# Seven of the last convolution tile's 31 taps made on TensorE as products with diagonal matrices

## The chip, the cores and the metric

The program runs on one core of one Trainium2 chip. The metric is the device time of one execution in microseconds (us). Engines: PE is TensorE, DVE is VectorE, ACT is ScalarE, POOL is GpSimd, and SP is SyncE, which issues the DMAs here. PE's clock has two levels, 1.2 and 2.4 GHz; the profile gives the granted clock as a share of the higher one (PEclk 0.50 or 1.00).

## What is computed

A trunk of two layers over 512 latent and 256 context tokens of width 1024. Layer 0 mixes tokens with a Conformer convolution module, layer 1 with windowed attention; behind each stands a mixture of experts. The change lies in the convolution module of layer 0:

```python
CONV_WIDTH = 31
def depthwise_conv(u, w, b, pad):
    y = lax.conv_general_dilated(u, w[:, None, :].astype(u.dtype), window_strides=(1,), padding=[pad],
                                 dimension_numbers=('NWC', 'WIO', 'NWC'), feature_group_count=u.shape[-1])
    return y + b.astype(u.dtype)

def conformer_conv(h, pw1, pw1_b, dw, dw_b, ln_g, ln_b, pw2, pw2_b):
    u = h @ pw1 + pw1_b
    u = u[..., :D_MODEL] * jax.nn.sigmoid(u[..., D_MODEL:])
    half = (CONV_WIDTH - 1) // 2
    u = depthwise_conv(u, dw, dw_b, (half, half))
    u = jax.nn.silu(layernorm(u, ln_g, ln_b))
    return u @ pw2 + pw2_b
```

Each channel is convolved along the tokens with its own 31 weights, all in float32. The layer norm behind it needs the mean and the variance over all 1024 channels, so its first step can't end before the last channel's convolution has.

## The kernel before

The channels lie on the partitions. There are 8 tiles (`KT`) of 128 channels, and a row of a tile has 783 columns (`CONVW`): 256 of context, a gap of 15, and 512 latent ones. Each engine has its own program, and semaphores order them.

**Pairs and loops.** Tiles go in pairs, `j` = 0 and 1 of pair `i` = 0 to 3. Pair 0 is written out; pairs 1 to 3 are a loop in each engine's program (`Fori`), where addresses and semaphore values come from registers.

**DVE.** `both_glu` (two instructions of L1302) multiplies the gate into the padded tile `UP`. `taps` then makes 31 instructions over 783 columns, one a tap: L1316, L1319, then 29 of L1321. Even taps add up in the tile's row block of `V` (shown as AR), odd ones in `ACC2` (shown as ROWS), and L1342 adds the two and raises `conv_done`. `mod_columns` follows the last tile (L443, L451: ten small instructions on the modulation columns), then eight of L1371 subtract the mean (`centred`).

**PE.** Per pair the pointwise product (`first_conv`, L1201), then `sum_mods`: five chunks of the modulation weights, each 2 MB by DMA into a slot of `RING`, as 32-column products (L426) and small ones that turn the sums (L433). After the loop stand the channel sums of tiles 0 to 5 (`add_mean`, L1225, two matmuls a tile: 512 and 271 columns with a matrix of ones), the last `sum_mods`, the channel sums of tiles 6 and 7, two transposes (`mod_rows_turn`, L457), and the sums of squares of all 8 tiles (L1249).

**ACT.** Sigmoids, the copies of the modulation sums out of PSUM (`copy_part`, L1258), then the squares (L1285), a square root (L1287) and the SiLU (L1290).

After the norm, L1377 (mean square out of PSUM), L1380 (reciprocal) and L1383 (scale, `scaled`) run on DVE; PE starts the second pointwise product (L861) with ACT's results, and SP starts six row loads (L470) and the first expert weights (L710) behind `scaled`. L1064 on DVE takes the first of those rows.

PSUM columns 1024 to 1806 (banks 2 and 3) hold the sums of squares (`VAR`) and, earlier, some modulation sums. Slot 2 of `RING` holds the second modulation chunk of each pair.

Of the kernel before, what the change touches and what calls it, by code (L numbers as in the profile page):

```python
# [24 lines left out]
P = 128  # L25
# [101 lines left out]
def build(nc, a, out):  # L127
    with ExitStack() as stack:
# [161 lines left out]
        pw_in = [sem(f"pw_in{j}") for j in range(2)]  # L290
        ctx_summed = sem("ctx_summed")
        ctx_sig_done = sem("ctx_sig_done")
        gate_summed = sem("gate_summed")
        val_summed = sem("val_summed")
        sig_done = sem("sig_done")
# [852 lines left out]
        VAR = PSF[:, 1024:1024 + CONVW]  # L1148
        NSTEP = 2 * (1 + TAPS)
        PART_BANK = (6, 2, 6, 2, 6)  # L1150


        MODS = [(0, 2 * KT + 4 * c, 2) for c in range(2)] + [(1, 4 * c, 3) for c in range(3)]
# [6 lines left out]
        with nc.Block() as block:  # L1160
# [32 lines left out]
            @block.tensor  # L1193
            def _(pe):
                def first_conv(i, j):
                    pe.wait_ge(pw_in[j], i * 32 + 32)
                    pe.wait_ge(glu_done[j], i + 1)
                    for (t0, lat, n, _), u, done in ((segs[0], 0, None), (segs[0], 1, ctx_summed),
                                                     (segs[1], 0, gate_summed), (segs[1], 1, val_summed)):
                        for k in range(KT):  # L1200
                            ins = pe.matmul(conv_bank(j, u, lat), PWB[:, j, u, k, :], HT[:, k, t0:t0 + n],  # L1201
                                            start=(k == 0), stop=(k == KT - 1))
                        if done:
                            ins.then_inc(done, 1)

                def add(i, c):
                    L, at, m = MODS[c]
                    pe.wait_ge(part_copied, i * 5 + (5 + c))
                    mod_rows_add(pe, L, i * (4 * m) + at, c)

                def sum_mods(i):
                    if not isinstance(i, int):
                        pe.wait_ge(glu_done[0], i + 3)
                    for c in range(len(MODS)):
                        if c >= 2:
                            add(i, c - 2)
                        pe.wait_ge(modB_in[c], i * 16 + (32 if c < 4 else 16))
                        mod_rows_sum(pe, PART_BANK[c], slot(1 + c, KT))
                    for c in range(len(MODS) - 2, len(MODS)):
                        add(i, c)  # L1220

                def add_mean(f):
                    pe.wait_ge(conv_done, f + 2)
                    for c0, c1 in ((0, 512), (512, CONVW)):
                        ins = pe.matmul(MEAN[:, c0:c1], ones[:, :], V[:, f, c0:c1], start=(f == 0), stop=(f == KT - 1))  # L1225
                    return ins

                for j in range(2):
                    first_conv(0, j)
                with pe.Fori(1, KT // 2) as i:  # L1230
                    for j in range(2):
                        first_conv(i, j)
                    sum_mods(i - 1)
                pe.wait_ge(glu_done[0], KT // 2 + 1)
                for f in range(KT - 2):
                    add_mean(f)
                sum_mods(KT // 2 - 1)
                pe.wait_ge(part_turned, 5 + 4 * len(MODS))
                pe.sem_inc(mod_summed[1], 1)
                for f in range(KT - 2, KT):  # L1240
                    ins = add_mean(f)
                ins.then_inc(mean_summed, 1)
                mod_rows_turn(pe, 0)
                mod_rows_turn(pe, 1)

                for f in range(KT):
                    pe.wait_ge(squared, f + 1)
                    for c0, c1 in ((0, 512), (512, CONVW)):
                        ins = pe.matmul(VAR[:, c0:c1], ones[:, :], SQ[:, f % 2, c0:c1],  # L1249
                                        start=(f == 0), stop=(f == KT - 1))  # L1250
                    ins.then_inc(sq_used, 1)

            @block.scalar
            def _(act):
                def copy_part(i, c):
                    act.wait_ge(part_summed, i * 5 + (5 + c))
                    act.wait_ge(part_turned, i * 5 + (1 + c))
                    nc.scalar.activation(PARTS[:, c, :], PS[:, PART_BANK[c], :], ACT.Copy).then_inc(part_copied, 1)  # L1258

                def sigmoid(i, j, seg, done):  # L1260
                    t0, lat, n, _ = seg
                    nc.scalar.activation(SGT[:, j, t0:t0 + n], conv_bank(j, 0, lat), ACT.Sigmoid,
                                         bias=cols[:, bass.ds(i * 2 + (VC["conv_pw1_b"] + KT + j), 1)]).then_inc(done, 1)

                def gates(i):
                    for j in range(2):
                        act.wait_ge(ctx_summed, i * 2 + (j + 1))
                        act.wait_ge(glu_done[j], i + 1)
                        sigmoid(i, j, segs[0], ctx_sig_done)
                        act.wait_ge(gate_summed, i * 2 + (j + 1))  # L1270
                        act.sem_inc(act_step, 1)
                        sigmoid(i, j, segs[1], sig_done)

                gates(0)
                with act.Fori(1, KT // 2) as i:
                    gates(i)
                    for c in range(len(MODS)):
                        copy_part(i - 1, c)
                for c in range(len(MODS)):
                    copy_part(KT // 2 - 1, c)  # L1280
                for f in range(KT):
                    act.wait_ge(centred, f + 1)
                    if f >= 2:
                        act.wait_ge(sq_used, f - 1)
                    nc.scalar.activation(SQ[:, f % 2, :], V[:, f, :], ACT.Square).then_inc(squared, 1)  # L1285
                act.wait_ge(var_ready, 1)
                nc.scalar.activation(STD, STD, ACT.Sqrt).then_inc(std_ready, 1)  # L1287
                for f in range(KT):
                    act.wait_ge(scaled, f + 1)
                    nc.scalar.activation(V[:, f, :], V[:, f, :], ACT.Silu,  # L1290
                                         scale=cols[:, VC["conv_ln_g"] + f:VC["conv_ln_g"] + f + 1],
                                         bias=cols[:, VC["conv_ln_b"] + f:VC["conv_ln_b"] + f + 1]).then_inc(z_ready, 1)

            @block.vector
            def _(dve):
# [49 lines left out]
                def first_tile(n):  # L1345
# [10 lines left out]
                    nc.vector.tensor_tensor(vf, vf, more, ALU.add).then_inc(conv_done, 1)  # L1356
                    return n

                n = first_tile(1)
                n = tile(0, 1, 0, n)  # L1360
                with dve.Fori(1, KT // 2) as i:
                    base = dve.snap(i * NSTEP + (n - NSTEP))
                    m = tile(i, 0, base, 0)
                    tile(i, 1, base, m)
                dve.wait_ge(mod_summed[1], 1)
                mod_columns(dve, 0, 2, NMOD)
                mod_columns(dve, 1, 0, NMOD)
# [799 lines left out]
```

## Time and profile before

| | us |
|---|---|
| median of 3 runs | 1571.44 |
| lowest, highest | 1570.62, 1572.45 |
| the profiled execution | 1571.96 |
| its span | 1570.2 |
| PE busy | 1348.2 |
| DVE busy | 757.1 |
| ACT busy | 508.3 |

Time points are us from the span's start. The convolution module takes the stretch to about 357 us. PE's share of the whole says little about it: there DVE is busy almost without a break and PE waits.

A float32 matmul is shown as two MATMUL and two LDWEIGHTS records, so the four matmuls of two channel sums are x8. In a merged row of the timeline the duration runs from the first start to the last end.

### The profile page before, as it was taken

Reading aid. Unit: us, or ns where it says so; the run is one execution under the profiler, and the core shown is the slowest. Engines: PE = TensorE matmul, PEld = TensorE weight load, DVE = VectorE, ACT = ScalarE, POOL = GpSimd, SP = SyncE. Lnnn points to the kernel's source line nnn. Section 1 sums busy time; section 2 is a strip of 40 time slices with the busy share of each in tenths; the row PEclk is TensorE's granted clock in tenths of the full one; section 3 lists DMA queues with packets and bytes.
Section 4 is the critical chain, followed back from the end, with each engine's and each line's share of the span. In section 5 each row is a group of like instructions: output and inputs, shape, how many; then the busy total and the mean of one; then the engine's idle time right before and its main releaser. Section 6 shows DMA issues by size and latency. Waiting matters only on the chain. (4 is left out here: it accounts for less than half of the span.)

```text
span 1570.2 us, 22957 instructions
## 1 busy us (share of the span) xinstructions
PE 1348.2 (86%) x6818; PEld 625.1 (40%) x6819; DVE 757.1 (48%) x1405; ACT 508.3 (32%) x783; POOL 126.7 (8%) x176
## 2 busy tenths in 40 slices
PE   4899998477978899999998299799998698998980
PEld 2555563234443233333332144378744332332320
DVE  2699999955773221221211541366647342232215
ACT  3101000042323443443332330166523253453423
POOL 0000000000320010010100200000002100100002
PEclk9999999778988999999999699899999799999995
DMA  9825473616049999699633500050094899999915
GB/s 345 286 73 198 156 268 136 251 59 252 40 181 341 396 398 375 238 329 333 240 116 126 216 0 0 5 104 1 1 335 144 307 337 395 397 370 397 359 33 194
DMA packets 163826, 342.97 MB, mean 218 GB/s; under 512 B 9104, under 2 KB 34304, under 8 KB 163776
## 3 DMA queue, kind: packets, MB, share of 16 engines
q1 hardware_dynamic: 146448, 298.29, 52.5%
q0 software_dynamic: 7440, 25.43, 4.4%
q10 hardware_dynamic: 9888, 18.62, 3.5%
q8 instruction: 27, 0.44, 0.1%
q14 instruction: 23, 0.19, 0.0%
HBM read 312.07 MB, written 30.24 MB: 218 GB/s over the span
## 5 line engine op out<-in xcount | busy, mean ns | idle before, releaser
L1485 PE MATMUL PS<-WR,XT 128*64 128x512 f32 x1760 | 414.1, 614 | 29.8 <-DVE WR L1618 20.2
L1485 PEld LDWEIGHTS PS<-WR,XT 128*64 128x64 f32 x1760 | 127.5, 140 | 266.0 <-issue 208.2
L1630 DVE TENSOR_TENSOR HID<-PS,SIL 64x512 f32<-64x512 f32 x55 | 37.5, 682 | 393.6 <-ACT SIL L1562 393.6
L1498 PE MATMUL PS<-WR,HTT 128*64 128x512 f32 x880 | 204.6, 608 | 9.5 <-ACT HTT L1567 9.5
L1551 ACT ACTIVATE WR<-WR 128x2048 f32 x90 | 169.0, 1906 | 100.5 <-issue 88.9
L1201 PE MATMUL PS<-HT,RING 128*128 128x512 f32 (+1 forms) x512 | 169.3, 494 | 6.5 <-DVEq L1299 6.5
L1618 DVE COPY WR<-WR 128x2048 f32 x90 | 107.0, 1224 | 97.9 <-PE PS L1498 40.3
L1201 PEld LDWEIGHTS PS<-HT,RING 128*128 128x128 f32 x512 | 99.4, 195 | 74.2 <-issue 66.3
L1321 DVE SCALAR_TENSOR_TENSOR AR<-AR,cols 128x783 f32 (+3 forms) x135 | 126.5, 937 | 0.0
L1321 DVE SCALAR_TENSOR_TENSOR ROWS<-AR,cols,ROWS 128x783 f32<-128x783 f32 (+2 forms) x126 | 118.0, 936 | 0.0
L1498 PEld LDWEIGHTS PS<-WR,HTT 128*64 128x64 f32 x880 | 59.4, 139 | 110.1 <-issue 106.6
L861 PE MATMUL PS<-RING,AR 128*128 128x512 f32 x192 | 93.0, 627 | 9.3 <-ACT AR L1290 9.3
L1799 PE MATMUL PS<-RING,HT 128*128 128x512 f32 x224 | 99.7, 603 | 1.3 <-ACT ROWS L1836 1.3
L1562 ACT ACTIVATE SIL<-PS 64x512 f32<-64x512 f32 x55 | 32.7, 594 | 116.4 <-PE PS L1485 116.4
L2040 DVE CUSTOM_DVE_ANT_0 HT<-PS,AR 128x512 f32<-128x512 f32 (+1 forms) x64 | 49.8, 815 | 33.9 <-PE PS L1964 33.9
L426 PE MATMUL PS<-RING,sc 128*32 128x512 f32 x384 | 51.8, 670 | 14.2 <-DMA RING<-in_w_mod 9.2
L1799 PEld LDWEIGHTS PS<-RING,HT 128*128 128x128 f32 x224 | 42.8, 194 | 52.9 <-issue 52.9
L861 PE MATMUL PS<-RING 128*128 128x512 f32 x128 | 60.2, 614 | 2.5 <-PEq L1940 2.5
L1574 ACT ACTIVATE YO<-PS 128x512 f32<-128x512 f32 x55 | 32.3, 587 | 89.6 <-PE PS L1498 89.6
L715 POOL DMA_INDIRECT XG<-moe_in,icur x57 | 55.7, 977 | 42.7 <-POOL icur L1451 41.5
L1567 ACT ACTIVATE HTT<-PS 128x256 f32<-128x256 f32 x55 | 20.6, 375 | 109.1 <-issue 59.9
L944 POOL TENSOR_SCALAR AR<-CN,HT 128x64 f32<-128x64 f32 x16 | 15.3, 959 | 501.8 <-DVEq L1035 501.8
(234 smaller groups left out, 1307.4 us busy)
## 6 DMA issues: line engine op xcount, KB each, us to landing
WR<-in_moe_w SPq DMA_DIRECT2D x192, 1024.0 KB, 15.6
RING<-in_w_mod SPq DMA_DIRECT2D x24, 2048.0 KB, 15.0
moe_out<-YO ACTq DMA_DIRECT2D x110, 128.0 KB
RING<-in_conv_pw SPq DMA_DIRECT2D x16, 512.0 KB, 5.4
moe_out<-HT SPq DMA_DIRECT2D x16, 512.0 KB, 8.7
ROWS<-rows_of_layer SPq DMA_DIRECT2D x12, 512.0 KB, 6.0
RING<-in_attn_w_qkv SPq DMA_DIRECT2D x3, 2048.0 KB, 8.5
RING<-in_conv_pw SPq DMA_DIRECT2D x2, 2048.0 KB, 9.7
```

Source lines behind the costliest of these rows:

```text
L426: ins = pe.matmul(PS[g:g + 32, bank, :], sc2[:, k, :], w[:, k, :], start=(k < 4), stop=(k >= 4), tile_position=(0, g))
L715: pool.indirect_dma_start(out=XG[:, :], out_offset=None, in_=src, in_offset=bass.IndirectOffsetOnAxis(ap=icur[:, 0:1], axis=0)).then_inc(x ...
L861: ins = pe.matmul(PS[:, 2 * (i % 2) + h, :], lhs(i, k), weights(k)[:, h * 512:(h + 1) * 512], start=(k == 0), stop=(k == KT - 1))
L1201: ins = pe.matmul(conv_bank(j, u, lat), PWB[:, j, u, k, :], HT[:, k, t0:t0 + n], start=(k == 0), stop=(k == KT - 1))
L1321: ins = nc.vector.scalar_tensor_tensor(out=to, in0=u, scalar=w, in1=to, op0=ALU.mult, op1=ALU.add)
L1485: ins = pe.matmul(PUV[g * SUB:(g + 1) * SUB, :], XT[:, k, :], w[:, k * FE:(k + 1) * FE], start=(k == 0), stop=(k == KT - 1), tile_position ...
L1498: ins = pe.matmul(PYO[c * SUB:(c + 1) * SUB, :], HTT[:, k, :], W2[:, at:at + 512], start=(k == 0), stop=(k == FE // P - 1), tile_position= ...
L1551: return nc.scalar.activation(to, src, ACT.Copy)
L1618: return nc.vector.tensor_copy(to, src)
L1630: nc.vector.tensor_tensor(HID[:, :], PUV[0:SUB, :], SIL[:, :], ALU.mult).then_inc(hid_ready[L], 1)
L1799: ins = pe.matmul(PS[:, bank, :], HT[:, k, t * P:(t + 1) * P], slot(QKV_SLOT[c], KT)[:, k, :], start=(k == 0), stop=(k == KT - 1))
L2040: nc.vector.tensor_tensor_reduce(out=SS[:, 2 * (s % 3) + b, 0:w], in0=PSF[:, 1024 * b:1024 * b + w], in1=mask, scale=-DH ** -0.5, scalar=n ...
```

## The change

Taps 24 to 30 of the last tile (pair 3, `j` = 1) leave DVE. ACT writes seven diagonal matrices of 128 by 128 (`DIAG`, in slot 2 of `RING`), each the identity scaled by that tap's weight column. PE multiplies each with the shifted 783 columns of `UP`, two matmuls a tap, and adds them up in PSUM banks 2 and 3 (`TAPSUM`). DVE makes 24 taps, adds its two accumulators, waits for `taps_summed`, and adds `TAPSUM`; that second addition raises `conv_done`.

To give the last tile a form of its own, DVE's loop now ends with pair 2, and pair 3 is written out. PE's and ACT's loops are as before.

```diff
+        PE_TAPS = 7
+        DIAG = RING[:, 2, 0:PE_TAPS * P].rearrange("p (k n) -> p k n", k=PE_TAPS)
+        TAPSUM = PSF[:, 1024:1024 + CONVW]
...
                 pe.sem_inc(mod_summed[1], 1)
-                for f in range(KT - 2, KT):
-                    ins = add_mean(f)
+                add_mean(KT - 2)
+                pe.wait_ge(ctx_sig_done, KT + 1)
+                pe.wait_ge(glu_done[1], KT // 2 + 1)
+                for k in range(PE_TAPS):
+                    at = TAPS - PE_TAPS + k
+                    for c0, c1 in ((0, 512), (512, CONVW)):
+                        ins = pe.matmul(TAPSUM[:, c0:c1], DIAG[:, k, :], UP[:, 1, at + c0:at + c1],
+                                        start=(k == 0), stop=(k == PE_TAPS - 1))
+                ins.then_inc(taps_summed, 1)
+                ins = add_mean(KT - 1)
                 ins.then_inc(mean_summed, 1)
...
                 for c in range(len(MODS)):
                     copy_part(KT // 2 - 1, c)
+                for k in range(PE_TAPS):
+                    w = DW + (TAPS - PE_TAPS + k) * KT + KT - 1
+                    ins = nc.scalar.activation(DIAG[:, k, :], ident, ACT.Copy, scale=cols[:, w:w + 1])
+                ins.then_inc(ctx_sig_done, 1)
...
+                def last_tile(n):
+                    i, j = KT // 2 - 1, 1
+                    n = both_glu(i, j, 0, n)
+                    n, (vf, more) = taps(i, j, 0, n, 0, CONVW, TAPS - PE_TAPS)
+                    nc.vector.tensor_tensor(vf, vf, more, ALU.add).then_inc(conv_step, 1)
+                    dve.wait_ge(conv_step, n + 1)
+                    dve.wait_ge(taps_summed, 1)
+                    nc.vector.tensor_tensor(vf, vf, TAPSUM, ALU.add).then_inc(conv_done, 1)
...
-                with dve.Fori(1, KT // 2) as i:
+                with dve.Fori(1, KT // 2 - 1) as i:
                     base = dve.snap(i * NSTEP + (n - NSTEP))
                     m = tile(i, 0, base, 0)
                     tile(i, 1, base, m)
+                n += (KT // 2 - 2) * NSTEP
+                n = tile(KT // 2 - 1, 0, 0, n)
+                last_tile(n)
```

PE, behind the last modulation chunk (L433 before, L434 in the change). Before, the channel sums of tiles 6 and 7 (L1225) and the two transposes (L457):

```order
L433 MATMUL PS<-CN,ROWS 128x2 x3
L1225 MATMUL PS<-AR,ones 128x512 [waits mod_part_turned,conv_done]
L1225 MATMUL PS<-AR,ones 128x271
L1225 MATMUL PS<-AR,ones 128x512 [waits conv_done]
L1225 MATMUL PS<-AR,ones 128x271
L457 MATMUL PS<-CN,modc 96x128 [waits mod_cols0]
```

The change, the same place (L1229 is the channel sum, L1250 a tap; 14 rows of L1250 in all):

```order
L434 MATMUL PS<-CN,ROWS 128x2 x3
L1229 MATMUL PS<-AR,ones 128x512 [waits mod_part_turned,conv_done]
L1229 MATMUL PS<-AR,ones 128x271
L1250 MATMUL PS<-AR,RING 128x512 [waits glu_done1,ctx_sig_done]
L1250 MATMUL PS<-AR,RING 128x271
...
L1250 MATMUL PS<-AR,RING 128x512
L1250 MATMUL PS<-AR,RING 128x271
L1229 MATMUL PS<-AR,ones 128x512 [waits conv_done]
L1229 MATMUL PS<-AR,ones 128x271
```

Between the two channel sums now stand 14 matmuls, ahead of the one that waits for the last tile.

DVE, the end of the last tile. Before, the last two taps (L1321) with a register instruction ahead of each, the sum of the accumulators (L1342), the loop's branch, and `mod_columns` (L443):

```order
L1311 REGISTER_ALU
L1321 ISA [waits conv_step]
L1321 SCALAR_TENSOR_TENSOR ROWS<-AR,cols,ROWS 128x783
L1311 REGISTER_ALU
L1321 ISA [waits conv_step]
L1321 SCALAR_TENSOR_TENSOR AR<-AR,cols 128x783
L1325 REGISTER_ALU
L1342 TENSOR_TENSOR AR<-AR,ROWS 128x783 [waits conv_step]
L1361 REGISTER_ALU
L1361 COMPARE_AND_BRANCH
L443 TENSOR_TENSOR modc<-PS,cols 128x32 [waits mod_summed1]
```

The change, the same place (L1337 is a tap, L1379 the sum of the accumulators, L1382 the addition of PE's part):

```order
L1337 SCALAR_TENSOR_TENSOR AR<-AR,cols 128x783 [waits conv_step]
L1337 SCALAR_TENSOR_TENSOR ROWS<-AR,cols,ROWS 128x783 [waits conv_step]
L1379 TENSOR_TENSOR AR<-AR,ROWS 128x783 [waits conv_step]
L1382 TENSOR_TENSOR AR<-AR,PS 128x783 [waits taps_summed,conv_step]
L444 TENSOR_TENSOR modc<-PS,cols 128x32 [waits mod_summed1]
```

The register instructions are gone, and one addition with a wait for PE has come.

## Rows read from the trace of the kernel before

**Rows 1.** Waits by engine and line, 255 to 360 us: total, times, longest

```profile
PE PS L1225 <- DVE AR L1342: 17.5, 1, 17.5
...
DVE RING L1064 <- DMA ROWS<-rows_of_layer: 11.8, 1, 11.8
...
DVE ROWS L1377 <- PE PS L1249: 6.1, 1, 6.1
...
DVE AR L1371 <- PE PS L1225: 1.1, 1, 1.1
```

**Rows 2.** Timeline of DVE, last tile, in the loop: start, duration, line

```profile
281.69 1.14 DVE L1302 SCALAR_TENSOR_TENSOR AR<-PS,cols,ROWS 128x256 f32<-128x256 f32 x2
283.20 0.69 DVE L1316 TENSOR_SCALAR AR<-AR,cols 128x783 f32 x1 [0.37 <-DVE AR L1302]
284.04 0.63 DVE L1319 TENSOR_SCALAR ROWS<-AR,cols 128x783 f32<-128x783 f32 x1 [0.15 <-DVE AR L1316]
284.58 1.03 DVE L1321 SCALAR_TENSOR_TENSOR AR<-AR,cols 128x783 f32 x1
...
311.03 1.03 DVE L1321 SCALAR_TENSOR_TENSOR AR<-AR,cols 128x783 f32 x1
312.10 0.97 DVE L1342 TENSOR_TENSOR AR<-AR,ROWS 128x783 f32 x1
```

**Rows 3.** Timeline of DVE, the second tile, written out, and the next tile's start

```profile
94.28 1.14 DVE L1302 SCALAR_TENSOR_TENSOR AR<-PS,cols,ROWS 128x256 f32<-128x256 f32 x2
96.72 1.03 DVE L1321 SCALAR_TENSOR_TENSOR AR<-AR,cols 128x783 f32<-128x783 f32 x1
...
125.14 1.14 DVE L1302 SCALAR_TENSOR_TENSOR AR<-PS,cols,ROWS 128x256 f32<-128x256 f32 x2
```

**Rows 4.** Timeline of PE, 268 to 341 us

```profile
268.55 8.15 PE L1225 MATMUL PS<-AR,ones 128*128 128x512 f32 x24
...
290.00 1.92 PE L426 MATMUL PS<-RING,sc 128*32 128x512 f32 x16 [2.45 <-DMA RING<-in_w_mod]
...
293.95 1.67 PE L1225 MATMUL PS<-AR,ones 128*128 128x512 f32 x4
313.12 2.98 PE L1225 MATMUL PS<-AR,ones 128*128 128x512 f32 x4 [17.50 <-DVE AR L1342]
315.89 0.63 PE L457 MATMUL PS<-CN,modc 128*96 128x128 f32 x2
318.05 13.02 PE L1249 MATMUL PS<-AR,ones 128*128 128x512 f32 x32 [1.53 <-ACT AR L1285]
340.36 10.14 PE L861 MATMUL PS<-RING,AR 128*128 128x512 f32 x16 [9.28 <-ACT AR L1290]
```

**Rows 5.** Busy time by stretch: length, PE, PEld, DVE, ACT, POOL; then PEclk, DMA share, GB/s

```profile
148.50:151.90 3.40, 3.40 (x10) 2.65 (x9) 3.40 (x5) 0.00 (x0) 0.00 (x0) 0.50 1.04 386
...
246.60:250.80 4.20, 0.00 (x0) 0.00 (x0) 4.17 (x7) 0.00 (x0) 0.00 (x0) 1.00 0.00 0
...
251.70:257.70 6.00, 6.00 (x32) 1.40 (x32) 5.64 (x7) 0.60 (x1) 0.00 (x0) 0.50 0.00 0
...
293.90:295.20 1.30, 1.25 (x4) 0.68 (x4) 1.30 (x3) 0.00 (x0) 0.00 (x0) 1.00 0.23 25
295.20:295.60 0.40, 0.40 (x2) 0.00 (x0) 0.40 (x1) 0.00 (x0) 0.00 (x0) 0.58 0.23 92
...
318.05:322.50 4.45, 4.45 (x6) 2.19 (x7) 4.45 (x6) 1.69 (x2) 0.00 (x0) 0.50 0.00 0
322.50:331.10 8.60, 8.58 (x27) 4.57 (x25) 2.49 (x8) 5.56 (x6) 0.00 (x0) 1.00 0.04 11
```

**Rows 6.** ACT: its last copy (timeline), and two 128x128 forms: busy, mean ns

```profile
292.00 0.60 ACT L1258 ACTIVATE ROWS<-PS 128x512 f32<-128x512 f32 x1 [4.76 <-PE PS L426]
...
L495 ACT ACTIVATE HT<-PS,modc 128x128 f32<-128x128 f32 x24 | 9.0, 456 | 16.8 <-PE PS L539 16.8
...
L934 ACT ACTIVATE HT<-PS 128x128 f32<-128x128 f32 x10 | 2.7, 274 | 5.0 <-PE PS L821 5.0
```

**Rows 7.** Timeline of DVE behind the last tile

```profile
314.32 0.77 DVE L451 SCALAR_TENSOR_TENSOR modc<-modc,cols 128x8 f32<-128x8 f32 x4
316.14 7.13 DVE L1371 SCALAR_TENSOR_TENSOR AR<-PS,AR 128x783 f32<-128x783 f32 x8 [1.05 <-PE PS L1225]
...
331.19 0.97 DVE L1377 TENSOR_SCALAR ROWS<-PS 128x783 f32<-128x783 f32 x1 [6.10 <-PE PS L1249]
```

**Rows 8.** Timeline of SP's queue and of DVE behind the norm

```profile
345.41 3.35 SPq L470 DMA_DIRECT2D ROWS<-rows_of_layer  x6
...
357.14 2.49 DVE L1064 TENSOR_TENSOR RING<-RING,ROWS 128x1024 f32<-128x1024 f32 x2 [11.81 <-DMA ROWS<-rows_of_layer]
```

More of the change, by code:

```diff
@@ L292, in build @@
         ctx_sig_done = sem("ctx_sig_done")
+        taps_summed = sem("taps_summed")
         gate_summed = sem("gate_summed")
```

## The prediction, on record before the result

> **What bounds the kernel now.** I read the waits by engine first, for the stretch that ends with the norm. PE waits 17.5 us for the last tile's sum (L1342) and DVE waits there for next to nothing [rows 1]. So the end of the convolution is DVE's alone, and what DVE saves on its last tile moves everything behind it. Then the timeline of DVE: the last tile's gate stands at 281.69, its taps 3 to 31 start at 284.58 to 311.03, 29 of them, and its sum ends at 312.10 + 0.97 = 313.07 [rows 2]. One tap costs (311.03 - 284.58) / 28 = 0.945 us. Then PE's timeline: the channel sum of tile 6 ends at 293.95 + 1.67 = 295.62, and nothing follows until 313.12 [rows 4]. That is the gap which the seven products go into. It opens at a fixed point, since the last modulation chunk waits for its DMA (L426 at 290.00, 2.45 us idle ahead of it) [rows 4].
>
> Behind the last tile come, in a row: the small modulation instructions on DVE, which end at 314.32 + 0.77 = 315.09; a wait of 1.05 us for the last channel sum; the subtraction of the mean from 316.14 [rows 7]; the sums of squares on PE, 13.02 us from 318.05 [rows 4], for which DVE waits 6.1 us [rows 1]; the norm; and then the row loads that SP issues at 345.41, for which DVE waits 11.8 us until 357.14 [rows 8]. SP issues them behind `scaled`, the last step of the norm, so this transfer starts earlier by whatever the norm ends earlier. I found no transfer in this chain that starts at a time of its own.
>
> **DVE, removed and moved.** Seven taps go: 7 x 0.945 = 6.61 us, all on the path. Pair 3 leaves the loop. A tile in the loop shows idle gaps of 0.37 and 0.15 us ahead of its first two taps, and runs from gate to third tap in 284.58 - 281.69 = 2.89 us [rows 2]. The written-out tile has no such gaps and needs 96.72 - 94.28 = 2.44 us [rows 3]. Two tiles now have the second form: 2 x 0.45 = 0.90 us. The interval of the taps does not change with it: the written-out tile takes 125.14 - 94.28 = 30.86 us [rows 3], 0.44 us under a tile of the loop, which is that start alone. The longer straight code could cost a fetch of instructions; the second tile is such code and shows no gap, so I take nothing. DVE's sum of the two accumulators would then end at 313.07 - 6.61 - 0.90 = 305.56.
>
> **DVE, added.** One addition of 783 columns with an operand in PSUM, behind the end of the first one. The subtraction of the mean is the same shape with the same operand places, 7.13 / 8 = 0.89 us of one behind another [rows 7]; an addition within SBUF is 0.97 us from start to end [rows 2]. Here each must have ended before the next starts, so I take 1.0 us, with 0.9 and 1.1 as ends.
>
> **ACT, added.** Seven copies of 128 columns with a scale, behind its last modulation copy, which ends at 292.60. No row shows this form; the nearest are 0.274 us (plain, out of PSUM) and 0.456 us (with scale and bias) [rows 6]. That makes 1.9 to 3.2 us, so the matrices are ready at 294.5 to 295.8. PE gets there at 295.62. Cost nothing, or 0.2 us in PE's gap. ACT has nothing else to do until 317.
>
> **PE, added.** A tap is a float32 product of 128 rows by 512 and 271 columns, the same form as a channel sum, and the weight load is the same too. Six channel sums took 8.15 us at the full clock, beside DVE's taps, so 1.36 us each, and seven taps 9.5 us [rows 4]. They would end at 305.1, half a us before DVE asks. But the clock: in the profile it falls at about 295.2, in the middle of the channel sum (1.00 up to 295.20, then 0.58 over the next 0.40 us) [rows 5]. What PE did before were small products, not nothing. The same happened at 148.5, where it fell while PE was busy and came back 3.4 us later [rows 5]. The seven taps start inside such a cold stretch. How long is it? With PE busy from its first moment on, 3.4 us as at 148.50, of which 3.0 lie behind 295.62: half of that is lost, 1.5 us, and the taps end at 306.6. The longest case in these rows is 6.0 us, from 251.70 to 257.70 [rows 5], 3.0 us lost and an end at 308.1. I take the first, because there too the engine had dense products when the clock fell; the 251.70 stretch followed 4.2 us of idleness.
>
> The Trainium skill ("TensorE: Matmul & The Clock Gate", section "HAM oscillation — how this bites in real kernels") lets the clock go back to half only after the engine has sat idle for long. By that rule the taps would run at the full clock, and the time would be that of the first rival below. The row at 293.90 to 295.60 speaks against it, since PE was busy for nearly all of it.
>
> So DVE waits 306.6 - 305.6 = 1.0 us for the taps, adds, and `conv_done` comes at 307.7 in place of 313.07: **5.4 us earlier**. The bounds are 306.6 with no wait (6.5 us) and 309.1 with the long cold stretch (4.0 us).
>
> **PE, behind it.** Queued behind the taps on PE are the last channel sum, the two transposes and the sums of squares. All wait for DVE anyway. Two of them get a warmer clock. The last channel sum took 2.98 us cold, and with the taps just ahead of it takes 1.4 to 1.7, as at 293.95 [rows 4]. It then ends before DVE's modulation instructions, so the wait of 1.05 us [rows 7] goes: **1.0 us**, not more, because those instructions are late next. The sums of squares began cold and ran so for 4.45 us, after which the rest went at the full clock [rows 5]; wholly warm they would be 2.2 us shorter. DVE's wait of 6.1 us there shows that PE is last, and ACT's squares and DVE's small work are covered by 3.9 us even then. But between the last channel sum and the first square lie 2.5 us with only two transposes, as sparse as the work before 295.2, and the clock may fall again: with 3.4 us cold the gain is (4.45 - 3.4) / 2 = 0.5. I take the middle, **1.4 us**. The ends are 2.2 and, with 6.0 us cold, a loss of 0.8.
>
> Behind the norm PE starts L861 cold or warm; that is covered by the 11.8 us in which everyone waits for the rows.
>
> **The sum.** 5.4 + 1.0 + 1.4 = 7.8 us. Against the profiled execution that is 1571.96 - 7.8 = 1564.2; against the median, which lies 0.5 lower, 1571.44 - 7.8 = **1563.6**.
>
> **Rivals.**
> - *Warm throughout.* The clock doesn't fall ahead of the taps, nor ahead of the squares: 6.5 + 1.0 + 2.2 = 9.7, 1561.7. For it: the fall at 295.2 lay at the very end of the sparse stretch, and a little shift could miss it. Against it: the trace has the fall. 20%.
> - *A long cold stretch under the taps.* 6.0 us, DVE waits 2.5 us: 4.0 + 1.0 + 1.4 = 6.4, 1565.0. 15%.
> - *PE becomes the bound (slower).* The clock stays low through all seven taps: 7 x 2 x 1.36 = 19.0 us from 295.6, an end at 314.6, `conv_done` at 315.6, 2.5 us later than before, with the channel sum as cold as it was: 1573.9. If the squares too stay cold for 6.0 us, 1574.7. It decides from the point where the taps end after 312.1. For it: PE is cold in the whole gap now. Against it: it is cold there while it does nothing, and each stretch of dense products in rows 5 got the clock back within 6.0 us. 8%, half of it beyond the bound of what can be told.
> - *The gain is swallowed behind the norm*, by a transfer that starts when it did: 1571.4. Against it: the row loads wait for `scaled`, and so do the expert weights behind them on SP's queue. 7%.
>
> **How the numbers follow.** My forecast has 50%. A measurement of this kernel can tell about 0.2%, 3.1 us, from no change. The forecast and the first two rivals are beyond it, 85%; the swallowed gain and half of the slow rival within, 11%; the other half slower, 4%. The range takes in the forecast's bounds: 6.5 + 1.0 + 2.2 = 9.7 (1561.7) and 4.0 + 1.0 - 0.8 = 4.2 (1567.2), and 0.6 us on either side for the spread of the runs (1570.62 to 1572.45): 1561.1 to 1567.8. That leaves the last two rivals out, 15%.
>
> **What would show it.** In the profile of the changed kernel: 24 taps on the last tile with 0.945 us between them; gate to third tap in 2.44 us on the last two tiles; seven small ACT rows over before 296; 28 tap records on PE from about 295.6 to 306.6 and PEclk at 0.50 for the first 3 us of them; a DVE wait for PE of about 1.0 us ahead of the new addition, and none ahead of the subtraction of the mean; that subtraction at 309.7 in place of 316.14, and the row loads at about 337.6 in place of 345.41. The forecast is wrong if the taps on PE cost more than a channel sum, if DVE's taps slow down while PE reads the same tile, or if the distance from the row loads to the end of the span is not what it was.

## The result, and the profile after

| | runs | median us | lowest, highest |
|---|---|---|---|
| before | 7 | 1571.09 | 1567.52, 1575.23 |
| the change | 7 | 1563.72 | 1560.04, 1567.97 |

The ratio is 0.995, with a 95% interval of 0.9938 to 0.9963: 5.8 to 9.7 us less. The forecast was 1563.6, 7.8 us less. The profiled execution took 1560.04 with a span of 1558.3, the fastest of its seven, so it shows more than the typical gain. One run of the kernel before, among those measured beside filler12 and early9, took 1695.75 us with a granted clock of 0.811 where the others had 0.923 to 0.931; it is left out of every median and ratio here.

The timeline of PE in the changed kernel (start, duration, line), which answers to [rows 4]. L427 and L434 are the last modulation chunk, L1229 channel sums, L1250 the taps, L1261 the sums of squares:

```profile
289.28 3.32 PE L427 MATMUL PS<-RING,sc 128*32 128x512 f32 x16 [2.44 <-DMA RING<-in_w_mod]
292.53 2.19 PE L434 MATMUL PS<-CN,ROWS 128*128 128x2 f32 x16
294.87 1.56 PE L1229 MATMUL PS<-AR,ones 128*128 128x512 f32 x4
296.26 9.38 PE L1250 MATMUL PS<-AR,RING 128*128 128x512 f32 x28
307.20 1.58 PE L1229 MATMUL PS<-AR,ones 128*128 128x512 f32 x4 [1.55 <-DVE AR L1382]
...
311.11 10.80 PE L1261 MATMUL PS<-AR,ones 128*128 128x512 f32 x32 [1.53 <-ACT AR L1301]
```

Seven taps took 9.38 us, 1.34 each. The last channel sum took 1.58 in place of 2.98, the squares 10.80 in place of 13.02. The timelines of DVE and of ACT there, which answer to [rows 2, 6, 7]:

```profile
281.82 1.14 DVE L1318 SCALAR_TENSOR_TENSOR AR<-PS,cols,ROWS 128x256 f32<-128x256 f32 x2
...
284.26 1.02 DVE L1337 SCALAR_TENSOR_TENSOR AR<-AR,cols 128x783 f32<-128x783 f32 x1
...
304.10 1.03 DVE L1337 SCALAR_TENSOR_TENSOR ROWS<-AR,cols,ROWS 128x783 f32<-128x783 f32 x1
305.17 0.97 DVE L1379 TENSOR_TENSOR AR<-AR,ROWS 128x783 f32<-128x783 f32 x1
306.18 0.97 DVE L1382 TENSOR_TENSOR AR<-AR,PS 128x783 f32<-128x783 f32 x1
...
309.20 7.12 DVE L1399 SCALAR_TENSOR_TENSOR AR<-PS,AR 128x783 f32<-128x783 f32 x8
...
322.02 0.97 DVE L1405 TENSOR_SCALAR ROWS<-PS 128x783 f32<-128x783 f32 x1 [3.88 <-PE PS L1261]
```
```profile
293.14 2.14 ACT L1295 ACTIVATE RING<-CN,cols 128x128 f32<-128x128 f32 x7
```

From the gate to the third tap are 284.26 - 281.82 = 2.44 us (2.89 in [rows 2]). 21 intervals from 284.26 to 304.10 give 0.945 us a tap, as before, though PE reads the same tile. The new addition (L1382) starts 1.01 us behind the first one and waits for nobody: the taps had ended at 305.64. The subtraction of the mean (L1399) has no wait ahead of it. ACT's matrices were ready at 295.28.

Busy time by stretch (length, PE, PEld, DVE, ACT, POOL, then PEclk, DMA share, GB/s), which answers to [rows 5]:

```profile
289.70:293.10 3.40, 3.40 (x19) 1.00 (x11) 3.40 (x5) 0.46 (x1) 0.00 (x0) 0.50 0.00 0
293.10:325.00 31.90, 25.20 (x85) 14.19 (x84) 26.58 (x42) 12.27 (x19) 0.00 (x0) 1.00 0.40 152
```

The clock fell here too, but at 289.7, under the modulation chunk, and was up from 293.1 on, 3.2 us ahead of the taps. That is not where the forecast had it, and the experiments turn on it.

**The measure used below.** Where pair 3 begins differs by up to 1.6 us between executions (250.1 to 251.7, shift7 aside, which moves it on purpose), and what lies behind the norm differs too. So each profile is read from the start of pair 3's first gate on DVE (250.40 before, 250.96 in the change) to the subtraction of the mean and to the mean square (L1377, L1405): 65.74 and 80.79 us before, 58.24 and 71.06 in this profile.

### The profile page after: what moved, and what is told of

It reads as the page before. It is cut to its first block and busy times, and to the rows that moved or that the text cites. A ratio compares the mean times of both kernels' runs of the same rounds, so it can differ in the third digit from the quotient of the medians.

```text
span 1558.3 us, 22883 instructions
## 1 busy us (share of the span) xinstructions
PE 1348.6 (87%) x6846; PEld 627.5 (40%) x6847; DVE 751.6 (48%) x1399; ACT 509.9 (33%) x790; POOL 126.7 (8%) x176
## 5 line engine op out<-in xcount | busy, mean ns | idle before, releaser
L1337 DVE SCALAR_TENSOR_TENSOR AR<-AR,cols 128x783 f32 (+3 forms) x131 | 122.4, 934 | 0.0
L1337 DVE SCALAR_TENSOR_TENSOR ROWS<-AR,cols,ROWS 128x783 f32<-128x783 f32 (+2 forms) x123 | 114.9, 934 | 0.0
L427 PE MATMUL PS<-RING,sc 128*32 128x512 f32 x384 | 50.1, 650 | 14.3 <-DMA RING<-in_w_mod 9.2
L1274 ACT ACTIVATE ROWS<-PS,cols 128x256 f32<-128x256 f32 (+1 forms) x16 | 9.3, 580 | 143.9 <-PE PS L1205 143.9
```

The lines of the kernel that those rows point to most:

```text
L427: ins = pe.matmul(PS[g:g + 32, bank, :], sc2[:, k, :], w[:, k, :], start=(k < 4), stop=(k >= 4), tile_position=(0, g))
L1337: ins = nc.vector.scalar_tensor_tensor(out=to, in0=u, scalar=w, in1=to, op0=ALU.mult, op1=ALU.add)
```

## The experiments

Each row of the table is one profiled execution; the texts follow. "To mean" is from pair 3's gate to the subtraction of the mean, "squares" from there to the mean square, "wait" DVE's wait for PE's taps, and "clock low" the stretches between 286 and 322 us in which PE's clock was at 0.50, or what of them lay there. The ratios are to the runs of before that were made beside that kernel. before_again and shift7 have none, because each was executed once (1569.91 and 1567.56 us).

| kernel | to mean | squares | wait | clock low | ratio (95%) |
|---|---|---|---|---|---|
| before | 65.74 | 15.05 | | 295.3-322.0 | |
| before_again | 65.75 | 12.83 | | 289.8-293.2, 300.0-317.1 | |
| unrolled_only | 64.85 | 14.28 | | 290.5-293.9, 300.7-321.2 | 0.9994 (0.9981-1.0007) |
| filler12 | 64.74 | 12.82 | | 288.8-292.2 | 0.9985 (0.9975-0.9995) |
| taps3 | 63.02 | 12.83 | 0 | 290.8-301.0, 307.9-314.7 | 0.9974 (0.9962-0.9986) |
| the change | 58.24 | 12.82 | 0 | 289.7-293.1 | 0.9950 (0.9938-0.9963) |
| again7 | 58.24 | 12.82 | 0 | 289.7-293.1 | 0.9951 (0.9931-0.9970) |
| again7_b | 61.08 | 14.49 | 2.87 | 290.4-300.6, 314.2-317.7 | 0.9944 (0.9927-0.9962) |
| shift7 | 58.85 | 14.53 | 0.66 | 297.7-301.1, 314.7-318.2 | |
| taps10 | 61.60 | 12.82 | 6.22 | 289.4-292.8 | 0.9977 (0.9966-0.9988) |
| early9 | 58.21 | 12.82 | 1.89 | 295.1-298.5 | 0.9939 (0.9922-0.9957) |
| early9_b | 56.95 | 14.51 | 0.64 | 294.4-297.9, 311.5-314.9 | 0.9944 (0.9927-0.9961) |
| early8 | 57.78 | 14.28 | 0 | 306.8-313.6 | 0.9945 (0.9925-0.9965) |
| early8_bridge | 57.31 | 12.82 | 0 | 294.9-298.3 | 0.9927 (0.9906-0.9947) |

### The change and the kernel before, profiled again

> The changed kernel again, for a second look at the clock. Measure: from the first gate of pair 3 on DVE (250.40 before, 250.96 in the first profile of the change) to the subtraction of the mean and to the mean square (L1371 and L1377 before; 65.74 and 80.79 us there, 58.24 and 71.06 in the first profile of the change). Theory A (mine): DVE's own saving is fixed, 6.6 + 0.9 - 1.0 = 6.5 us, and the clock adds to it: 0 to 1.0 us at the subtraction and up to 2.2 us more at the mean square, because PE is no longer idle ahead of them. Where the clock falls, in the small products ahead of the taps or within the taps, differs from one execution to the next. So 58.2 to 60.8 to the subtraction, 71.0 to 75.6 to the mean square, and a time 7.4 us below before, with 1.5 us of uncertainty. Theory B: the clock's part in the first profile was that execution's luck, and a second one shows the cold sums of before, 59.3 and 74.3 us, and about 6.5 us in time.

> The kernel before, for a second look at its clock. Its sums of squares took 15.05 us from the subtraction of the mean to the mean square in the first profile, with 4.45 us of them cold; with the pair 3 written out and nothing else changed 14.28, with the change 12.82. Theory A: PE is idle for 17 us ahead of the last channel sum in each execution, so that sum takes 2.98 us and DVE waits 1.05 us; the squares take 13 to 15 us, by where the clock comes back. Theory B: the 15.05 was luck and the squares are as often warm: 12.8.

The second profile of the change repeated the first to 0.01 us, and the median of the runs was 1563.16 (before 1572.47). The second profile of before gave half of each theory: the last channel sum took 2.98 us again, and DVE waited 1.05 us for it, but the squares were as quick as in the change. DVE's timeline in that second profile of before:

```profile
316.80 7.13 DVE L1371 SCALAR_TENSOR_TENSOR AR<-PS,AR 128x783 f32<-128x783 f32 x8 [1.05 <-PE PS L1225]
329.63 0.97 DVE L1377 TENSOR_SCALAR ROWS<-PS 128x783 f32<-128x783 f32 x1 [3.88 <-PE PS L1249]
```

So the 1.05 us belong to the kernel before, and the 15.05 us of squares were that execution's. The third profile of the change, taken beside the later versions, was unlike the other two:

> The changed kernel, beside the versions below on the same chip. Theory A: 58.24 us from the gate of pair 3 to the subtraction of the mean where the clock is up in the taps, up to 59.8 where it falls there; 12.82 to 14.5 us on to the mean square; 7 to 8 us below before.

```profile
289.67 3.02 PE L427 MATMUL PS<-RING,sc 128*32 128x512 f32 x16 [2.45 <-DMA RING<-in_w_mod]
292.62 3.57 PE L434 MATMUL PS<-CN,ROWS 128*128 128x2 f32 x16
296.34 2.95 PE L1229 MATMUL PS<-AR,ones 128*128 128x512 f32 x4 [0.15 <-PE PS L434]
299.08 10.14 PE L1250 MATMUL PS<-AR,RING 128*128 128x512 f32 x28
```
```profile
290.40:300.60 10.20, 10.05 (x34) 5.89 (x27) 10.20 (x11) 2.63 (x8) 0.00 (x0) 0.50 0.31 109
```
```profile
305.48 0.97 DVE L1379 TENSOR_TENSOR AR<-AR,ROWS 128x783 f32<-128x783 f32 x1
309.33 0.97 DVE L1382 TENSOR_TENSOR AR<-AR,PS 128x783 f32<-128x783 f32 x1 [2.87 <-PE PS L1250]
```

(PE's timeline, the stretch, and DVE's timeline of this third profile.) The clock was low for 10.2 us with PE busy for 10.05 of them. The taps themselves lost only 0.8 us; they began at 299.08 in place of 296.26, because the small products ahead of them ran at half speed (3.57 us in place of 2.19, the channel sum 2.95 in place of 1.56). DVE waited 2.87 us. The median was 1564.34 against 1570.93, over six runs of which the profiled one, at 1570.75, was the slowest.

### What DVE saves by itself

> DVE's loop ends with pair 2 and pair 3 is written out, all 31 taps stay on DVE, PE and ACT are as before. Theory A: the idle gaps ahead of the first two taps go on two tiles, 0.90 us: 64.8 us from the gate of pair 3 to the subtraction of the mean (65.74 before), a time 0.9 us lower, which the runs can hardly tell from none. PE is idle as before, so it is cold at the last channel sum, and DVE's 1.05 us wait stays. Theory B, that the longer straight code costs fetches of instructions: gaps of their own ahead of some taps of pair 3, and 65.7 us or more.

```diff
-                with dve.Fori(1, KT // 2) as i:
+                with dve.Fori(1, KT // 2 - 1) as i:
                     base = dve.snap(i * NSTEP + (n - NSTEP))
                     m = tile(i, 0, base, 0)
                     tile(i, 1, base, m)
+                n += (KT // 2 - 2) * NSTEP
+                n = tile(KT // 2 - 1, 0, 0, n)
+                tile(KT // 2 - 1, 1, 0, n)
```

DVE's timeline with pair 3 written out:

```profile
282.33 1.14 DVE L1302 SCALAR_TENSOR_TENSOR AR<-PS,cols,ROWS 128x256 f32<-128x256 f32 x2
283.50 0.69 DVE L1316 TENSOR_SCALAR AR<-AR,cols 128x783 f32<-128x783 f32 x1
284.22 0.63 DVE L1319 TENSOR_SCALAR ROWS<-AR,cols 128x783 f32<-128x783 f32 x1
284.76 1.03 DVE L1321 SCALAR_TENSOR_TENSOR AR<-AR,cols 128x783 f32<-128x783 f32 x1
...
316.33 7.13 DVE L1374 SCALAR_TENSOR_TENSOR AR<-PS,AR 128x783 f32<-128x783 f32 x8 [1.05 <-PE PS L1225]
```

The two idle gaps of [rows 2] are gone: 64.85 us against 65.75, 0.90 less, and no gap for a fetch. The time doesn't tell 0.9 us from nothing (1571.66 against 1572.47), as expected. The wait of 1.05 us is still there.

### More and fewer taps

> The change with three taps on PE in place of seven. Theory A: DVE saves 3 x 0.945 + 0.9 - 1.0 = 2.7 us. PE's three products end at 299.7 and it is then idle for some 10 us, so its clock is low again at the last channel sum and the squares: 63.0 us from the gate of pair 3 to the subtraction of the mean with DVE's wait of about 1 us still there, 78 us to the mean square, and 2.7 us off the time. Theory B (the clock's gain doesn't depend on how full PE's gap is): the same wait is gone and the squares take 10.8 us, so 62.0 and 74.9 us, and 5.9 us off the time. Three against seven taps then tells apart DVE's 0.945 us a tap (3.8 us for four) from the clock's part (0 to 3.2 us on top).

> The change with ten taps on PE. Theory A: a tap costs PE 1.36 us at the full clock and starts behind tile 6's channel sum at 295.6, so ten end at 309.2 (1.5 to 3 us later with a cold stretch), while DVE is ready at 302.7: a wait of 6.5 us or more on DVE, the subtraction of the mean 61.9 us behind the gate of pair 3 (58.2 with seven), the mean square 74.7, and a time some 3 us over that of seven taps but 4 us under before. PE is the bound from eight taps on: 1.36 us a tap come where 0.945 go. If a tap cost PE less than that or DVE's taps slowed beside it, the subtraction would come under 60 us or the interval of DVE's taps would be over 0.945 us.

Both are the change with one number edited (`PE_TAPS = 3`, `PE_TAPS = 10`). Three taps: 63.02 us to the mean, theory A's number, with the wait of 1.06 us still ahead of the subtraction. Its squares took 12.83, theory B's. The stretches tell how: PE had nothing to do from 304.2 to 311.6, the clock fell in the middle of that at 307.9, so the last channel sum was cold, and the clock came back at 314.7, ahead of the squares. From three taps to seven the mean comes 63.02 - 58.24 = 4.78 us earlier: 4 x 0.945 + 1.0 for the warm channel sum. The times differ by 5.2 us (1568.38, and 1563.16 of the change beside it).

Ten taps, timelines of PE and DVE:

```profile
295.90 13.33 PE L1250 MATMUL PS<-AR,RING 128*128 128x512 f32 x40
```
```profile
302.14 0.97 DVE L1379 TENSOR_TENSOR AR<-AR,ROWS 128x783 f32<-128x783 f32 x1
309.34 0.97 DVE L1382 TENSOR_TENSOR AR<-AR,PS 128x783 f32<-128x783 f32 x1 [6.22 <-PE PS L1250]
```

1.33 us a tap on PE, 6.22 us of waiting, 61.60 us to the mean (61.9 expected), 3.4 us off the time of before (1569.03 against 1572.47). PE is the bound here, though its clock was up in all of the taps. The two lines cross at seven: PE's seven ended at 305.64, DVE's sum at 306.14.

### The clock alone

> The kernel before, with twelve channel-sum-like products of tile 7's padded rows (24 matmuls into PSUM columns that nobody reads) in PE's gap between the channel sums of tiles 6 and 7; DVE makes all 31 taps in its loop. The clock's part alone. Theory A: the fillers end at about 312, the last channel sum takes 1.6 us in place of 2.98, DVE's wait of 1.05 us goes (64.7 us from the gate of pair 3 to the subtraction of the mean), and the squares go from 13 to 15.05 us down to 12.82: 1.0 + 0.2 to 2.2 us, a time 1.2 to 3.2 us below before. Theory B: a filled gap changes nothing at the squares, since the clock falls again in the 2.5 us behind the last channel sum: 1.0 us and no more.

```diff
-                for f in range(KT - 2, KT):
-                    ins = add_mean(f)
+                add_mean(KT - 2)
+                pe.wait_ge(glu_done[1], KT // 2 + 1)
+                for k in range(12):
+                    for c0, c1 in ((0, 512), (512, CONVW)):
+                        pe.matmul(VAR[:, c0:c1], ones[:, :], UP[:, 1, c0:c1], start=(k == 0), stop=(k == 11))
+                ins = add_mean(KT - 1)
```

PE's timeline, and DVE's:

```profile
295.63 15.96 PE L1244 MATMUL PS<-AR,ones 128*128 128x512 f32 x48
313.25 1.58 PE L1225 MATMUL PS<-AR,ones 128*128 128x512 f32 x4 [1.66 <-DVE AR L1346]
```
```profile
315.25 7.12 DVE L1375 SCALAR_TENSOR_TENSOR AR<-PS,AR 128x783 f32<-128x783 f32 x8
```

With work for nobody in PE's gap the wait of 1.05 us goes (64.74 us to the mean in place of 65.75), and the squares take 12.82. The medians are 1569.51 against 1570.60, and by the interval the kernel takes 0.8 to 3.9 us less. The 1.0 us at the last channel sum is the part of the change's gain that has nothing to do with taps. Whether the filling also warms the squares is not shown: they took 12.83 in before_again without it, and a gain of 1.0 us (theory B) lies in the interval as well as theory A's.

### Where the clock falls

> The change with two fills of DVE's odd accumulator ahead of the second tile's taps, some 1.5 us that shift all that follows against the changes of PE's clock (both profiles of the change show the clock low at 289.7 to 293.1, ahead of the taps). The forecast had the clock fall at the end of the small products and the taps start cold. Theory A: where the clock falls depends only on where its changes lie against the work; shifted by 1.5 us, the last small products and the channel sum of tile 6 meet the next change, the clock falls between 293.5 and 296.5 and the first 3.4 us of the taps run at half speed: taps of 10.5 to 11 us in place of 9.38, a wait on DVE of 0.5 to 1.5 us ahead of PE's addition, 58.8 to 59.7 us from the gate of pair 3 to the subtraction of the mean in place of 58.24. Theory B: the products with diagonals keep the clock up in any case: 9.4 us and 58.24 again.

```diff
                 n = first_tile(1)
-                n = tile(0, 1, 0, n)
+                n = both_glu(0, 1, 0, n)
+                for _ in range(2):
+                    nc.vector.memset(ACC2[:, :], 0.0).then_inc(conv_step, 1)
+                    n += 1
+                    dve.wait_ge(conv_step, n)
+                n, (vf, more) = taps(0, 1, 0, n, 0, CONVW, TAPS)
+                nc.vector.tensor_tensor(vf, vf, more, ALU.add).then_inc(conv_done, 1)
```

Busy time by stretch, then the timelines of PE and DVE:

```profile
292.80:297.70 4.90, 4.75 (x35) 2.77 (x36) 4.90 (x6) 2.63 (x8) 0.00 (x0) 1.00 0.01 3
297.70:301.10 3.40, 3.40 (x7) 1.99 (x6) 3.40 (x5) 0.00 (x0) 0.00 (x0) 0.50 0.93 322
```
```profile
298.59 10.63 PE L1250 MATMUL PS<-AR,RING 128*128 128x512 f32 x28
```
```profile
309.32 0.97 DVE L1382 TENSOR_TENSOR AR<-AR,PS 128x783 f32<-128x783 f32 x1 [0.66 <-PE PS L1250]
```

This is the forecast's case: the clock falls within the channel sum of tile 6, with PE busy since 292.80, stays low for 3.4 us, and the taps take 10.63 us in place of 9.38. DVE waits 0.66 us, 58.85 us to the mean. The fall came at 297.7, 1.2 us later than expected; pair 3 had moved by 2.5 us and not by 1.5, and the last chunk's products by 3.5 (292.80 in place of 289.28). So the products with diagonals do not keep the clock up (theory B is out), and a fall beside the taps costs what the forecast said. That the shift brought the fall there is not shown: this is one execution, and again7_b had its cold stretch elsewhere with no shift at all. The squares show the same thing again (low from 314.7 to 318.2, 14.53 us).

### Eight and nine taps, two of them early

> The change with nine taps on PE: ACT writes the matrices behind its second modulation copy, two taps stand in PE's wait for the last modulation chunk (2.44 us idle at 286.8), seven ahead of tile 6's channel sum. Theory A: DVE is the bound up to where PE's taps end; PE's end at about 303 (52 us behind the gate of pair 3), DVE's two accumulators are added at 304.2 (53.3 us), so nobody waits: 58.24 - 2 x 0.945 = 56.35 us from the gate to the subtraction of the mean, 69.2 to the mean square, and a time 1.9 us below the change. Theory B: the modulation chunk's products, now behind two taps, end later than the 0.3 us I count, and the mod columns' sums hold up DVE: 57 us or more.

> Nine taps again. In its first profile the clock fell 5 us into the last stretch of small products and taps, DVE waited 1.89 us for PE, and the gain of the two more taps was gone (58.21 us). Theory A: with the clock up, 56.4 us; with it down, 58.2; which of the two is the execution's. The time lies beside that of eight taps within 1 us.

> As the version with nine taps, two of them in PE's wait for the last modulation chunk and the matrices written early, but eight in all. Nine had PE as the bound once the clock fell within the taps (11.14 us for seven, DVE waits 1.89). Theory A: with eight, six stand behind the small products; they end some 43 + 8.1 = 51.8 us behind the gate of pair 3 warm and 53.5 cold, DVE asks at 54.3 us, so DVE never waits: 58.24 - 0.945 = 57.3 us to the subtraction of the mean in either case, and a time about 1 us below the change and 8 to 9 below before. Theory B (early taps delay the chunk's products and with them something else): 58 us or more.

> As eight taps, with one product of 783 columns of loaded weights with the ones (2 matmuls, the result overwritten) on PE behind the two transposes, in its wait for the first square. It was to see whether the squares' cold start (14.53 us in the shifted kernel, 12.82 else) is that gap's doing. Theory A: the product ends before the first square or at most 0.3 us behind, and the squares are warm in every execution: 12.8 to 13.1 us from the subtraction to the mean square, a time 0 to 1 us below eight taps without it. Theory B: the clock falls there all the same, or the squares are as often warm without it: no difference, or 0.3 us more.

```diff
+                        if isinstance(i, int) and c == 4:
+                            pe.wait_ge(part_copied, i * 5 + (5 + 3))
+                            pe.wait_ge(ctx_sig_done, KT + 1)
+                            pe.wait_ge(glu_done[1], KT // 2 + 1)
+                            some_taps(0, EARLY)
                         pe.wait_ge(modB_in[c], i * 16 + (32 if c < 4 else 16))
...
+                some_taps(EARLY, PE_TAPS).then_inc(taps_summed, 1)
                 add_mean(KT - 2)
...
                     copy_part(KT // 2 - 1, c)
+                    if c == 1:
+                        for k in range(PE_TAPS):
...
```

(`some_taps(k0, k1)` makes PE's taps k0 to k1 - 1; the seven matrices' loop of ACT moves up with its count, and the change's own loop on PE is gone) and, for the bridge, behind `mod_rows_turn`:

```diff
+                pe.wait_ge(w_in[0], 32)
+                for c0, c1 in ((0, 512), (512, CONVW)):
+                    pe.matmul(VAR[:, c0:c1], ones[:, :], RING[:, 4, c0:c1], start=True, stop=True)
```

Nine taps (PE's timeline, and DVE's):

```profile
287.38 2.88 PE L1236 MATMUL PS<-AR,RING 128*128 128x512 f32 x8
290.19 1.93 PE L427 MATMUL PS<-RING,sc 128*32 128x512 f32 x16
292.04 1.95 PE L434 MATMUL PS<-CN,ROWS 128*128 128x2 f32 x16
294.14 11.14 PE L1236 MATMUL PS<-AR,RING 128*128 128x512 f32 x28
```
```profile
302.52 0.97 DVE L1387 TENSOR_TENSOR AR<-AR,ROWS 128x783 f32<-128x783 f32 x1
305.39 0.97 DVE L1390 TENSOR_TENSOR AR<-AR,PS 128x783 f32<-128x783 f32 x1 [1.89 <-PE PS L1236]
```

The early pair fills PE's wait for the DMA, the chunk's products start some 0.2 us later than behind an idle wait, and the seven taps behind them took 11.14 us, since the clock fell within them. DVE waited 1.89 us and the expected 56.35 became 58.21. The second profile gave 56.95 with a wait of 0.64. With nine, then, 0.6 to 1.9 of the 1.9 us gained are lost. The cold stretch doesn't explain the difference between the two, for the seven taps took 11.14 and 11.15 us. PE's last chunk does: its products started 290.19 - 250.21 = 39.98 us behind pair 3's gate in the first and 290.41 - 251.70 = 38.71 in the second.

Eight taps have no wait in either of their two profiles, the second (the bridge's) with a cold stretch in the taps: 57.31 us, the expected number. The first had 57.78: PE was idle for 3.47 us ahead of the last channel sum, the clock fell at 306.8, the sum took 2.46 us, and DVE waited 0.54 us for it. I had not counted that, and its squares were cold with 14.28. With the bridging product the squares took 12.82 and the median was the lowest of all, 1558.41 against 1570.93, 5.9 us under the change's 1564.34 beside it. The intervals of the two ratios, 0.9927 (0.9906 to 0.9947) and 0.9944 (0.9927 to 0.9962), overlap, so it is shown to beat the kernel before; that it beats the change is likely and not shown. Nor would the eighth tap explain 5.9 us: to the mean the version gained 0.9 us (57.31 for 58.24). One profile doesn't show that the squares are warm each time, nor that the bridging product warmed them: the clock had fallen at 294.9 here, as at 295.1 in early9, whose squares took 12.82 without it.

## Why the prediction was right, and where its steps were not

**What bounds the stretch, and that its gain is kept: right.** DVE's own saving came through whole. In the first profile of the change the mean square comes 80.79 - 71.06 = 9.7 us earlier, and the row loads still took 12.0 us of DVE's waiting ([rows 8] has 11.8). From the first use of these rows to the end of the span are 1213.06 and 1212.5 us in the two profiles of before, and 1210.1, 1213.0 and 1216.1 in the three of the change, 1213.1 on average: nothing was swallowed there and nothing added.

```profile
348.17 2.49 DVE L1065 TENSOR_TENSOR RING<-RING,ROWS 128x1024 f32<-128x1024 f32 x2 [12.00 <-DMA ROWS<-rows_of_layer]
```

**DVE's terms: right to 0.1 us.** 6.61 for the taps: 0.945 a tap on DVE in the change, and from three to seven taps 4.78 us, of which 1.0 is the channel sum's. 0.90 for the written-out pair, by unrolled_only. 1.0 for the added addition (1.01 us behind the first). Matrices ready at 295.28, within the bounds.

**The tap on PE: right.** 1.36 us forecast, 1.34 and 1.33 measured.

**The last channel sum: right.** 1.0 us, by filler12 alone and in each profile of the change.

**"DVE waits 1.0 us for the taps": the right size on average, by a step that doesn't hold.** The three profiles of the change have waits of 0, 0 and 2.87 us. None has the forecast's 1.0, and that they average to it is luck. The forecast said that PE's gap "opens at a fixed point", 295.62, and that only the taps in it run cold or warm. Its start depends on the clock as well, 296.26, 296.27 and 299.08, and on the DMA: counted from pair 3's gate, the last chunk's products started 39.60 us later in the first profile of before and 38.29 in the second. The small products of the last chunk are on PE's path, and in again7_b they and not the taps brought most of the delay. The bound that I set on a cold stretch from [rows 5], 6.0 us, was too short too: 10.2 us came twice (again7_b, taps3), with PE busy for 10.05 of them. The trace of before had longer ones outside [rows 5], as from 1008.7 to 1025.7, 17.0 us with PE busy for 10.9. For these reasons the rival with a long cold stretch, priced at 2.5 us of waiting, was 0.4 short of what came.

**The squares, 1.4 us: too much.** The term was taken against 15.05 us, one execution. The second profile of before had 12.83, and unrolled_only, in which PE is idle nearly as long (15.87 us for 17.50), 14.28: 14.1 on average. The three profiles of the change have 12.82, 12.82 and 14.49, 13.4 on average. That leaves 0.7 us, from so few profiles that it can't be told from nothing.

**The sum.** To the mean square, two profiles of before average 79.7 us and three of the change 72.6: 7.1 us. The medians of the runs say 7.4 and, in the two later comparisons, 9.3 and 6.6. So the forecast of 7.8 was the sum of DVE's exact terms, 7.5 with the channel sum, and of two clock terms, a wait and the squares, which nearly cancel. The first part is shown. That the total came so close owes something to luck, since each clock term is a mean of cases that differ by more than itself, and the time alone, 5.8 to 9.7 us less, wouldn't have told the forecast from the warm rival (9.7) or from the long cold one (6.4).

**The rivals.** Warm taps and squares, given 20%, is what the first two profiles show, though the clock did fall: it was back up 3 us ahead of the taps. PE as the bound is a matter of ten taps, not of the clock: even 10.2 us of low clock cost 2.87 us and not 9. Nothing was swallowed behind the norm.

**The rule in the Trainium skill** ("TensorE: Matmul & The Clock Gate", section "HAM oscillation — how this bites in real kernels"), by which the clock goes back after the engine has sat idle for long: the trace of shift7 disagrees. PE was busy for 4.75 of the 4.90 us ahead of the fall at 297.7. For two of them what it did were products of two columns (L434). Where PE had waited 2.44 us and the clock fell just behind (the change, 289.7), the rule's order of events is there, but for a wait of 2.44 us. The traces agree with the rule where PE waits longer: in the first profile of before the clock fell at 250.8, behind the 4.2 us of idle PE in [rows 5] and with PE still idle, and in taps3 it fell 3.7 us into PE's wait of 7.4. So a long wait stood ahead of the fall in these cases, and in shift7 the fall came without one.

**The spread.** The forecast counted 0.6 us on either side for the runs, from three of them. Seven runs of either kernel spread over 8 us. Part of it is in this stage (the mean square of the change lies 71.06 or 75.57 us behind the gate), part behind the row loads:

```profile
348.17:1558.30 1210.13, 1055.97 (x5588) 465.61 (x5588) 467.38 (x1032) 447.86 (x693) 126.30 (x170) 0.93 0.62 225
```
```profile
352.89:1569.00 1216.11, 1059.35 (x5588) 466.09 (x5588) 467.34 (x1032) 447.98 (x693) 125.87 (x170) 0.93 0.61 224
```

(Busy time from the first use of the loaded rows to the end, first and third profile of the change.) 6.0 us lie between them with the same instructions, PE busy 3.4 us longer and the other engines within 0.5. Over the seven runs of the change the time goes with the mean granted clock, from 0.937 in the fastest (1560.04 us) to 0.932 and 0.931 in the two slowest (1567.73 and 1567.97). Which of the two follows the other was not tested.

## What to carry to other kernels

Work moved from a bound engine into another's gap is worth its full time as long as the receiving side ends first: compute the crossing (1.34 us a tap on PE against 0.945 saved on DVE cross at seven). Where the receiver's speed is not constant, one below the crossing may be the better choice; six taps were not run. Give a TensorE gap's start the same doubt as its filling, since the small products ahead of it change pace with the clock too, and start when their DMA lands. Where an engine goes cold in a gap, filling it pays a second time at the first work behind it, here 1.0 us. Up to 2.2 us more lay in the squares, by the execution, and no run ties those to the filling.

## What the hardware showed that was not expected

- The clock went to half with PE almost fully busy, 1.1 us behind the 16 products of two columns (shift7, 297.7, for 3.4 us). In early9, early9_b and the bridge it fell at 295.1, 294.4 and 294.9, under the taps, 0.2 to 1.1 us behind the same 16 products. In the first profile of before, 295.3 is such a place too, and so is 148.5, 0.6 us behind the 16 such products of an earlier pair, with PE busy for 4.45 of the 4.50 us ahead. That the narrow products are the reason was not tested.
- Where it fell earlier, behind PE's 2.44 us of waiting for the last chunk, it came back after 3.4 us (the change, 289.7 to 293.1) or after 10.2 us with PE busy for 10.05 of them (again7_b, 290.4), with the same instructions in the same order.
- The same 16 products of two columns (L434) took 1.95 us at the full clock, and 3.57 in the low one.
- The same kernel has two faces in its profiles: 71.06 us to the mean square in two of them, to the hundredth, and 75.57 in the third.
